# Moving the activation rows 64 bytes within a 256-byte period, against a weight ring that stays

## The reference

```
h = rmsnorm(x, g)
x = x + attention(h @ w_qkv) @ w_out
x = x + (silu(h @ w_gate) * (h @ w_up)) @ w_down          # twice, then rmsnorm
...
x = x + gate * (concat(fourier, gated, attention) @ w_out)  # twice, with 256 context tokens
```

## The kernel before

| matmuls | moving | stationary | moving minus stationary |
|---|---|---|---|
| L180 to L182, weights stationary, 512 or 256 columns | 128 | 128 | 0 |
| L183 to L185, `tok`, 512 columns | 128 | 128 | 0 |
| L183 to L185, `bv` and window values, 256 columns | 64 | 128 | -64 |
| L180 to L182, `kr` (32 columns stationary) | 128 | 128 and 0 | 0 and 128 |

## Time and profile before

### The profile page before, as it was taken

The page is one execution under the profiler, slowest core; times in us unless marked ns, Lnnn a source line. Parts: engine busy times, 40 slices in busy tenths (PEclk is TensorE's granted clock), DMA queues, the critical chain, the costliest instruction groups (busy, mean ns, idle before and its releaser), DMA issues.

```text
span 2173.2 us, 30673 instructions
## 1 busy us (share of the span) xinstructions
PE 2145.1 (99%) x12586; PEld 1754.2 (81%) x12586; DVE 997.2 (46%) x1764; ACT 799.3 (37%) x1371; POOL 734.5 (34%) x339
## 2 busy tenths in 40 slices
PE   9999999999999999999999999999999999999999
PEld 8778888888889898888878888887886667886677
DVE  5664555541222333334465555345305673552672
ACT  6445333333333333334443333333225442334531
POOL 3116444455443333333174444443221002232102
PEclk9999999999999999999999999999999999999999
DMA  4103444432322222221034444322110001322002
GB/s 153 40 30 110 145 145 146 144 126 97 107 93 88 82 81 82 78 88 69 35 121 146 145 146 146 135 97 95 59 68 35 1 1 40 110 78 83 1 2 78
DMA packets 57659, 191.53 MB, mean 88 GB/s; under 512 B 8112, under 2 KB 11440, under 8 KB 57264
## 3 DMA queue, kind: packets, MB, share of 16 engines
q1 hardware_dynamic: 46128, 155.82, 20.6%
q10 hardware_dynamic: 11392, 33.75, 4.4%
HBM read 185.35 MB, written 2.10 MB: 86 GB/s over the span
## 4 chain that ended last, share of the span: by engine, by line
PE 88%; DVE 3%; ACT 1%; issue 1%; DVEq 1%; POOL 0%; ACTq 0%; POOLq 0%; DMA 0%
PE ps L180 21%; PE ps L181 21%; PE ps L182 21%; PE ps L2729 4%; PE ps L183 3%; PE ps L185 3%; PE ps L184 3%; PE ps L2761 2%; PE ps L2741 2%; PE ps L1105 2%; PE ps L1139 1%; PE ps L1121 1%; PE ps L2284 0%; PE ps L2250 0%; PE ps L2097 0%
## 5 line engine op out<-in xcount | busy, mean ns | idle before, releaser
L253 POOL TENSOR_TENSOR w_lo<-w_raw,w_hi 128x1024 fp32r<-128x1024 f32 x282 | 682.0, 2419 | 1332.2 <-ACT w_hi L170 1318.0
L170 ACT ACTIVATE w_hi<-w_raw 128x1024 fp32r<-128x1024 f32 x284 | 300.3, 1058 | 539.3 <-DMA w_raw<-in_wstream 539.0
L180 PE MATMUL ps<-h_hi,w_hi 128*128 128x512 f32 x1168 | 464.0, 397 | 2.7 <-DVE w_lo L295 1.8
L182 PE MATMUL ps<-h_hi,w_lo 128*128 128x512 f32 x1168 | 455.0, 390 | 0.0
L181 PE MATMUL ps<-h_lo,w_hi 128*128 128x512 f32 x1168 | 455.0, 390 | 0.0
L180 PEld LDWEIGHTS ps<-h_hi,w_hi 128*128 128x128 f32 x1168 | 219.3, 188 | 50.7 <-DVE w_lo L295 2.0
L182 PEld LDWEIGHTS ps<-h_hi,w_lo 128*128 128x128 f32 x1168 | 219.3, 188 | 46.0
L181 PEld LDWEIGHTS ps<-h_lo,w_hi 128*128 128x128 f32 x1168 | 219.5, 188 | 43.3 <-issue 0.7
L183 PE MATMUL ps<-w_hi,h_hi 128*128 128x256 f32 x416 | 116.6, 280 | 0.0
L185 PE MATMUL ps<-w_hi,h_lo 128*128 128x256 f32 x416 | 115.5, 278 | 0.0
L184 PE MATMUL ps<-w_lo,h_hi 128*128 128x256 f32 x416 | 115.5, 278 | 0.0
(11 more groups left out here) (362 smaller groups left out, 4019.5 us busy)
## 6 DMA issues: line engine op xcount, KB each, us to landing
w_raw<-in_wstream SPq DMA_DIRECT2D x283, 512.0 KB, 3.2
f0mod_rows<-in_wmod ACTq DMA_DIRECT2D x24, 512.0 KB, 4.6
f1mod_rows<-in_wmod ACTq DMA_DIRECT2D x24, 512.0 KB, 4.6
dvS<-dvE SPq DMA_DIRECT2D x64, 32.0 KB, 2.5
out<-x SPq DMA_DIRECT2D x8, 256.0 KB, 3.2
x<-in_x SPq DMA_DIRECT2D x3, 512.0 KB, 6.9
l_dft<-in_dft ACTq DMA_DIRECT2D x4, 384.0 KB, 4.2
l_wuq<-in_wuq ACTq DMA_DIRECT2D x2, 768.0 KB, 6.1
```

What stands on the lines that cost most here:

```text
L170: self.A.activation(self.slot(self.w_hi, n), self.slot(self.w_raw, n), ACT.Copy).then_inc(self.w_high, 1)
L180: T.matmul(out, wh, ah, start=start, stop=False)
L182: return T.matmul(out, wl, ah, start=False, stop=stop)
L253: G.tensor_tensor(c.slot(c.w_lo, n), c.slot(c.w_raw, n), c.slot(c.w_hi, n).bitcast(F32), ALU.subtract).then_inc(c.w_low, 1)
```

## The change

The rows of the stages move from 128 to 64 past a multiple of 256 bytes, and SHIFT goes from 48 elements (192 bytes) to 32 (128 bytes). `top` becomes 89920, 64 bytes lower. The ring and its slots stay where they are, and so do the fixed tiles. No instruction is added, removed or put elsewhere in any queue, and no size changes.

```
-SLOT, SHIFT = 1088, 48
+SLOT, SHIFT = 1088, 32
...
-        self.top = self.offset = (nc.sbuf_base + 127) // 256 * 256 + 128
+        self.top = self.offset = (nc.sbuf_base + 191) // 256 * 256 + 64
```

## The result

The changed kernel is slower: 2208.0 us, median of 4 runs, against 2172.53; the ratio is 1.0168, 95% interval 1.0154 to 1.0183. The forecast was 2166.3 us and the range 2138 to 2200, so the time lies outside it, on the side of the rival that had 34%.

A forecast was written before the change was run, and what follows sets the result against it. TensorE's matmul pace was taken as the only bound. Context rows -3.5, value blocks -1.7 and restarts -1.0 us sum to -6.2 us, taking 2172.5 to 2166.3 us, range 2138 to 2200.

The forecast's parts named there:

- the rival that had 34%: Every run of 512-column matmuls no longer settles at -64: 4.6 ns each, 27 us slower, about 2197 us; chance 34%.
- What bounds the kernel: Whole kernel: only TensorE's pace moves the time; matmuls in flight 99% of the span, 6.0 us per nanosecond of large-stream pace.
- the edits costed at nothing: DMAs, waits, elementwise work, GpSimd's subtraction, plain fp32 and transposes: no change in time expected, 0 us.
- The 5952 large ones: 0: 512-column matmuls moving from offset 0 to -64 keep 226.7 ns, taken as a floor; bounds 220.0 and 231.3 ns.
- Reading (b), the fixed sum: Surcharge is fixed per matmul, so 512 columns at -64 take 220.0 to 224.6 ns; about 2140 us, chance 18%.
- Context rows: -3.5 us: 528 matmuls of 256 context columns go from offset 0 to -64, from 120.0 to 113.3 ns each.
- Value blocks: -1.7 us: Of 26 blocks at -64, the 8 behind 512-column matmuls drop from 117.9 to 113.3 ns; other bound +3.9 us.
- Restarts: -1 us: Slow first five 512-column intervals after width changes, 27 ns each, some 70 restarts, near 2 us; half taken as saved.
- `tok`: 0: 240 matmuls of 512 columns going from offset 0 to +64: no change taken, between 0 and 1.1 us.
- The rival that nothing moves: Offset does nothing; 120.0 against 113.3 ns comes from whether weights or activations stream; 2172.5 us, chance 12%.

The follow-up runs named there:

- the second probe: Separate kernel without the computation: 48-matmul streams at varied load sizes, widths and offsets, plus plain fp32; only paces read, plain fp32 429.2 ns a pass at three offsets.
- the first probe: Separate kernel without the computation: 48 fp32r matmuls per offset and absolute place; 512 columns settle at 226.7 ns at offset 0, 233.3 at -64; time not comparable.
- the rows alone: Changed kernel with SHIFT left at 48, so only the stages' rows move: 2213.28 us, ratio 1.0181.
- the ring moved: Kernel before with rows kept at 128, ring and fixed tiles 64 bytes higher and SHIFT 32, giving the change's offsets: 2209.46 us, ratio 1.0166.
- the rows above: Kernel before with rows at 192 past a multiple of 256, 64 above the ring, and SHIFT 0: 2182.41 us, ratio 1.0039.

## Why the prediction was wrong

**What bounds the kernel** was right: the pace of TensorE, with the large streams weighted at 6.0 us a nanosecond. So were the edits costed at nothing: queues, GpSimd and plain fp32 did not move, the last shown by the second probe.

**The step that failed** is "The 5952 large ones: 0", with its reason that "-64 holds the floor once it is reached after a break". They settle at 233.3 ns, 6.2 ns above the 227.1 that they had on the mean with their restarts, and this term alone is +35.5 us in the table above, 5952 x 6.2 = 36.9 over all of them. Two inferences carried it and both fell. The first took 226.7 as a floor because it is 2 x 113.3; the widths between show no such proportion, and the equality is chance as far as these runs go. Had 226.7 been a floor, it would not have said that -64 reaches it. The second carried a fact about 256 columns, where -64 is better than 0, over to 512, where no row had it. The probe shows the opposite order for the two widths. Reading (b), the fixed sum, was right for offset 0 at these two widths and just as wrong about -64: both readings took one width's gain to bind the other.

**The rival that came true** had the right place and mechanism, streams of 512 columns that stay off their pace, and too small a price: 4.6 ns from the transients of the earlier trace rows and the block `kr` of the earlier trace rows, against 6.2. Those two rows were no measure of it. Transients at offset 0, and loads of 32 columns, with which the second probe shows 512 columns insensitive to the offset, are other cases. Its upper bound, 235.8 ns, held the value, and the range stopped at 2200 where that bound called for up to 2222. The forecast's own range, 2164 to 2173, was cut too narrow in the same way: its small terms at their bounds (-1.1, +3.9, 0 and +1.1) add up to 2176.

**Context rows: -3.5 us.** Measured -2.0. The lower pace was taken for all; ten of the thirteen runs of the first layer settle at 117.8, which I had put down to streams at offset 0 ahead of them. After the change none of those is left, and 117.8 is still there.

**Value blocks: -1.7 us.** Measured +1.0. Of the 8 blocks at 117.8 four went to 113.3, as forecast for all eight; of the 18 at 113.3 nine went to 117.8, half of the bound of +3.9. Their absolute place, at 0 and 64, does nothing by the first probe.

**Restarts: -1 us** came to nothing of its own, since at -64 the large streams stay at or about 233 ns and have no better pace to settle to. What they cost before, 227.1 against 226.7 ns over the large ones, is some 2.4 us, near the 2 of the estimate. **`tok`: 0** measured +0.5, at 229.3 ns, within its bound of 1.1.

**The rival that nothing moves** is refuted by four kernels (the changed one, the rows alone, the ring moved, the rows above) that differ from the one before in addresses alone. The Trainium skill, "SBUF — State Buffer", section Who interferes with whom, has TensorE's two read ports independent; by that rule the large streams would have kept their time, and the measurement disagrees, 233.3 ns against 226.7 for the same instructions.

## What to carry to other kernels

With a load for every matmul and fp32r at full rate, the place of the moving operand against the stationary one, modulo 256 bytes and down to 4, is worth up to 6% of the pace (239.9 ns against 226.7), and the best place for one width or load size can be among the worst for another. Don't carry a pace from one width, load size or preceding stream to the next: a loop of 48 matmuls for each offset costs 10 us of chip time and gives the value. Weigh such a term by its share first: here 62% of the span hung on one unmeasured number, and small gains on the other streams, 2 us, could never have paid for it.

## What the runs showed of the hardware

That a stream of identical matmuls keeps one of two paces for 48 instructions and longer, by how it was entered, was not expected: 113.3 or 117.8 ns for 256 columns at -64. Most of the streams whose intervals all agree to 1 ns have multiples of 6.67 ns, which is 16 cycles at 2.4 GHz: 113.3, 120.0, 146.7, 173.3, 226.7 and, at -64, 233.3. It is no rule: 256 columns at an offset of 32, behind a settled stream, hold 116.7 ns just as evenly. What sets these steps stays open.

Plain fp32 passes of 256 columns run at 215.8 ns at every offset tried. The Trainium skill, "TensorE: Matmul & The Clock Gate", section Back-to-back issue gap, has N / 2.4 + 2.5 ns for an isolated warm matmul. An estimate from it with two cycles a column is 215.8 ns, and the second probe agrees. For fp32r the same formula gives 109.2 ns at 256 columns and 215.8 at 512, again estimates, and no offset reached either: the lowest settled paces were 113.3 and 226.7 ns.
